# Block sums of a layer's up weights: made by accumulating transfers in DRAM instead of on GpSimd

## The reference, cut to what matters

```
h = h + mx[5] * conv_ffn(modulate(rmsnorm(h, norm2_g[1]), mx[3], mx[4]), w_up[1], conv_w[1], conv_b[1], w_down[1])
```

## Time and profile before

| | |
|---|---|
| time, median of 3 runs | 2627.46 us (2626.0 to 2628.0) |
| the profiled execution, its own time | 2625.86 us |
| its span, first to last instruction | 2624.1 us |
| TensorE busy | 2435.8 us, 93% |
| VectorE busy | 1433.1 us, 55% |
| ScalarE busy | 924.4 us, 35% |
| GpSimd busy | 527.5 us, 20% |
| traffic | 322.33 MB, mean 123 GB/s |
| mean granted TensorE clock | 0.984 of full speed |

### The profile page before, as it was taken

One profiled execution on the slowest core, in us unless ns is written; L12 is line 12 of the kernel. 1 busy time (PEld: TensorE's weight loads), 2 busy tenths in 40 slices (PEclk: granted clock), 3 DMA queues, 4 the chain that ended last, 5 costly groups with the idle time before them and its releaser, 6 DMA issues. The chain is left out here.

```text
span 2624.1 us, 35244 instructions
## 1 busy us (share of the span) xinstructions
PE 2435.8 (93%) x14592; PEld 1884.4 (72%) x14592; DVE 1433.1 (55%) x2132; ACT 924.4 (35%) x1524; POOL 527.5 (20%) x388
## 2 busy tenths in 40 slices
PE   6999999999999999999988878899899999998977
PEld 5887578888887887996667878674664578773323
DVE  4323664766667215226679989536766766532223
ACT  3224433332325114225445555423432653330001
POOL 0502320000001001105247667100013120012112
PEclk9999999999999999999999899999999999999999
DMA  6214901111111212127112222321110114458998
GB/s 241 78 65 142 335 27 60 54 65 65 65 60 45 67 58 79 65 81 272 71 65 81 73 72 76 122 89 74 65 61 10 49 49 145 161 219 352 417 412 331
DMA packets 63248, 322.33 MB, mean 123 GB/s; under 512 B 8109, under 2 KB 20397, under 8 KB 31789
## 3 DMA queue, kind: packets, MB, share of 16 engines
q1 hardware_dynamic: 51374, 300.27, 31.0%
q0 software_dynamic: 5696, 12.59, 1.3%
q10 hardware_dynamic: 6016, 7.18, 0.8%
HBM read 315.82 MB, written 12.58 MB: 125 GB/s over the span
## 5 line engine op out<-in xcount | busy, mean ns | idle before, releaser
L1750 PE MATMUL ps<-work_rounded,ring_rounded 128*128 128x512 f32 (+3 forms) x1968 | 518.4, 351 | 6.0 <-PEq L1555 3.6
L1750 PE MATMUL ps<-xn_rounded,ring_rounded 128*128 128x512 f32 (+3 forms) x2176 | 508.8, 345 | 0.0
L1750 PEld LDWEIGHTS ps<-xn_rounded,ring_rounded 128*128 128x128 f32 (+1 forms) x2176 | 349.2, 189 | 53.5 <-issue 0.5
L1750 PEld LDWEIGHTS ps<-work_rounded,ring_rounded 128*128 128x128 f32 (+1 forms) x1968 | 324.0, 189 | 62.7 <-issue 6.3
L1750 PE MATMUL ps<-big_rounded,ring_rounded 128*128 128x512 f32 (+1 forms) x1168 | 314.9, 356 | 11.3 <-DVE big_rounded L1650 8.7
L1650 DVE TENSOR_TENSOR ring_rounded<-ring,ring_rounded 128x2048 fp32r<-128x2048 f32 (+4 forms) x107 | 192.6, 1800 | 237.4 <-ACT ring_rounded L1614 237.3
L3048 PE MATMUL ps<-xn_rounded,ring_rounded 128*128 128x512 f32 (+1 forms) x1408 | 305.5, 339 | 0.0
L1614 ACT ACTIVATE ring_rounded<-ring 128x2048 fp32r<-128x2048 f32 (+4 forms) x107 | 161.0, 1505 | 309.9 <-PE ps L1750 281.6
L3048 PEld LDWEIGHTS ps<-xn_rounded,ring_rounded 128*128 128x128 f32 x1408 | 218.0, 189 | 30.9
L1750 PEld LDWEIGHTS ps<-big_rounded,ring_rounded 128*128 128x128 f32 x1168 | 190.7, 189 | 53.1 <-DVE big_rounded L1650 12.6
L798 PE MATMUL ps<-xn_rounded,ring_rounded 128*128 128x258 f32 x418 | 128.7, 308 | 35.1 <-DVE h_rounded L978 14.5
(11 more groups left out here) (534 smaller groups left out, 4293.5 us busy)
## 6 DMA issues: line engine op xcount, KB each, us to landing
ring<-in_stream SPq DMA_DIRECT2D x141, 1024.0 KB, 4.9
big<-in_experts SPq DMA_DIRECT2D x44, 1024.0 KB, 24.0
ring<-in_stream SPq DMA_DIRECT2D x32, 704.0 KB, 4.0
ring<-in_experts SPq DMA_DIRECT2D x17, 1024.0 KB, 27.3
xn<-in_experts SPq DMA_DIRECT2D x15, 1024.0 KB, 15.5
work<-in_experts SPq DMA_DIRECT2D x15, 1024.0 KB, 15.3
big<-in_first_modulation SPq DMA_DIRECT2D x8, 1024.0 KB, 14.8
work<-in_bias ACTq DMA_DIRECT2D x20, 256.0 KB, 4.2
```

The source lines that it names most:

```text
L1750: mm = pe.matmul(out[:, a - u.first:b - u.first], lhs, rhs, start=j == 0 and n == 0 and not u.onto, stop=j == terms - 1 and n == len(passe ...
```

## The change

1. The host lays the four blocks of all 22 strips out a second time, block by block (`blocks`, four arrays of 704 x 2048). In layer 0's `ffn_up`, POOL issues eight DRAM-to-DRAM transfers into a new tensor `block_sums`: four copies, then four that add onto what is there. POOL waits for completion three times between them. The scheme is now that of the matrix with its second half negated, so every sum is an addition: `block_sums` holds S1 = A21+A22, S2' = A11+S1, S3' = A11+A21 and S4' = A12+S2'. In return the activation sums T1, T2 and T4 are formed with the opposite sign (`minus_sum`), and the second half is multiplied by -1 where it is evicted.
2. In the stage, POOL makes no sums. SP loads them: a strip comes in three transfers (A11 with A12, A22, and S4' in A21's place), and S1, S2 and S3 in one of 256 KB each, when the product that used their place is done. S2 has two places now, S1 and S3 one.
3. The first half's convolution is held in a PSUM bank (`middle`) instead of SBUF: ACT's `centre` writes it there, DVE's two taps work on it there, `silu` reads it and writes SBUF.
4. The lists of DVE and ACT are in a new order.

```diff
@@ SevenProducts @@
-    def sum_s1(self, pool, n):
...
-        pool.tensor_tensor(self.sums(0, 2), pair(2), pair(3), ALU.add).then_inc(self.sums_made.up(), 1)
...
+    def first_loads(self, sp):
+        sp.wait_ge(b.blocks_summed.sem, b.all_blocks_summed)
+        b.load_strips_until(sp, self.first + 1)
+        for name, n in (("S1", 0), ("S2", 0), ("S3", 0), ("S2", 1)):
+            self.load_sum(sp, name, n)
+    def loads(self, sp):
+        for i in range(FT):
+            if i + 1 < FT:
+                sp.wait_ge(self.done.sem, self.after("P5", i))
+                self.load_sum(sp, "S1", i + 1)
+            if i + 2 < FT:
+                sp.wait_ge(self.done.sem, self.after("P6", i))
+                self.load_sum(sp, "S2", i + 2)
+            b.load_strips_until(sp, self.first + i + 3)
+            if i + 1 < FT:
+                sp.wait_ge(self.done.sem, self.after("P7", i))
+                self.load_sum(sp, "S3", i + 1)
...
     def gpsimd(self, pool):
         self.add_square(pool, KT - 1)
-        self.sum_s1(pool, 1)
-        self.sum_s2(pool, 1)
-        for i in range(FT + 1):
...
+        for i in range(1, FT + 1):
+            if i - 1 < FT - 1:
+                self.add_side(pool, i - 1)
+            if i >= 2:
                 self.gate(pool, i - 2)
...
     def silu(self, act, i):
         act.wait_ge(self.convolved.sem, self.convolved.at(3 * i + 2))
-        act.activation(self.cv[:, i % 2, 0, :], self.cv[:, i % 2, 0, :], ACT.Silu).then_inc(self.silued.up(), 1)
+        if i >= 2:
+            act.wait_ge(self.gated.sem, self.after_gate(i - 2))
+        act.activation(self.cv[:, i % 2, 0, :], self.middle(i), ACT.Silu).then_inc(self.silued.up(), 1)
...
     def make_fourth(self, dve, i):
...
+        if i >= 2:
+            dve.wait_ge(self.silued.sem, self.silued.at(i - 1))
...
     def convolve_first(self, dve, i, part):
-        cc, a = self.cv[:, i % 2, 0, :], 2 * part
+        cc, a = self.middle(i), 2 * part
@@ Builder.load_strips_until @@
+            if i in BLOCK_STRIPS:
+                sp.dma_start(room[:, 0:1024], strip[:, 0:1024]).then_inc(self.landed[slot], 16)
+                sp.dma_start(room[:, 1536:2048], strip[:, 1536:2048]).then_inc(self.landed[slot], 16)
+                sp.dma_start(room[:, 1024:1536], self.sum_of(3, n)).then_inc(self.landed[slot], 16)
+    def sum_blocks(self, pool):
+        for to, block in ((0, 2), (2, 0), (1, 0), (3, 1)):
+            pool.dma_start(sums[to], blocks[block]).then_inc(summed.up(16), 16)
+        pool.wait_ge(summed.sem, summed.now())
+        pool.dma_start(sums[0], blocks[3], accum_op=ALU.add, max_dma_last_dim=4 * STRIP).then_inc(summed.up(16), 16)
+        pool.dma_start(sums[2], blocks[2], accum_op=ALU.add, max_dma_last_dim=4 * STRIP).then_inc(summed.up(16), 16)
+        pool.wait_ge(summed.sem, summed.now())
+        pool.dma_start(sums[1], sums[0], accum_op=ALU.add, max_dma_last_dim=4 * STRIP).then_inc(summed.up(16), 16)
+        pool.wait_ge(summed.sem, summed.now())
+        pool.dma_start(sums[3], sums[1], accum_op=ALU.add, max_dma_last_dim=4 * STRIP).then_inc(summed.up(16), 16)
@@ ffn_up, on GpSimd @@
                 pool.memset(w[:, 0:4 * 772], 0.0).then_inc(zeroed.up(), 1)
+                self.sum_blocks(pool)
```

More of the change, by code:

```diff
@@ L115 @@
 WIDTH = [len(rows) // P * len(cols) for _, rows, cols in PLAN]
+BLOCK_STRIPS = [i for i, (name, _, _) in enumerate(PLAN) if name == ("w_up", DEPTH - 1)]
+TRANSFERS = [3 if i in BLOCK_STRIPS else 1 for i in range(STRIPS)]
 def pack_strip(matrix, rows, cols):
@@ L313, in lay_out @@
     out["first_modulation"] = np.stack([pack_strip(x["w_mod"][0], np.arange(D), np.arange(c, c + 256)) for c in range(0, 256 * MOD_FIRST, 256)])
+    blocks = np.stack([stream[i] for i, (name, _, _) in enumerate(PLAN) if name == ("w_up", DEPTH - 1)])
+    out["blocks"] = blocks.reshape(FT, P, 4, 512).transpose(2, 0, 1, 3).reshape(4, FT * P // 4, STRIP)
     experts = np.empty((EXPERTS, P, 3 * STRIP), np.float32)
@@ L548, in __init__ @@
             lows += [("s4_a22", i - 1)]
-            lows += [("s3", i), ("a12", i)] if i < FT else []
+            lows += [("a12", i), ("s3", i)] if i < FT else []
             lows += [("a11", i + 1)] if i + 1 < FT else []
+        added = [("side", 0)]
+        for i in range(1, FT - 1):
+            added += [("side", i), ("gate", i - 1)]
+        added += [("gate", FT - 2)]
+        self.added_number = {p: n + 1 for n, p in enumerate(added)}
         self.high_number = {p: n + 1 for n, p in enumerate(highs)}
@@ L733, in sum_s3, with load_sum @@
-    def sum_s3(self, pool, n):
-        self.b.strip(pool, self.first + n)
-        if n >= 2:
-            pool.wait_ge(self.done.sem, self.after("P7", n - 2))
-        pair = lambda part: self.slot(n, part).rearrange("p (k c) -> p k c", k=2)
-        pool.tensor_tensor(self.sums(4 + 2 * (n % 2), 2), pair(0), pair(2), ALU.subtract).then_inc(self.sums_made.up(), 1)
-    def sum_s4(self, pool, n):
-        pool.wait_ge(self.sums_made.sem, self.sum_number(n, "S2"))
-        pair = lambda part: self.slot(n, part).rearrange("p (k c) -> p k c", k=2)
-        pool.tensor_tensor(pair(2), pair(1), self.sums(2, 2), ALU.subtract).then_inc(self.sums_made.up(), 1)
+    def load_sum(self, sp, name, n):
+        which = ("S1", "S2", "S3").index(name)
+        place = self.sum_place(name, n)
+        landed = self.sum_landed[name + str(n % 2) if name == "S2" else name]
+        sp.dma_start(self.sums(place, 2), self.b.sum_of(which, n)).then_inc(landed, 16)
@@ L1056, in vector @@
         self.low_a12(dve, 0)
+        self.make_fourth(dve, 0)
         self.low_s3(dve, 0)
@@ L1112, in _ @@
             def _(sp):
-                b.load_strips(sp)
+                self.loads(sp)
             @block.scalar
@@ L2904, in _, with output_projection @@
                 normalise(2)
-    def output_projection(self, src, segments, residual, prefetch=None, add=None, gpsimd=None, next_sources=None, tiles_ahead=0, rooms=None, after=None, waiting=(1, 2)):
+    def output_projection(self, src, segments, residual, prefetch=None, add=None, gpsimd=None, next_sources=None, tiles_ahead=0, rooms=None, after=None, waiting=(1, 2), loads=None):
         width = segments[-1][1]
@@ L2929, in finish @@
             return ins
-        self.project(units, 4, finish, banks_each=2, prefetch=prefetch, add=add, gpsimd=gpsimd, after=after,
+        self.project(units, 4, finish, banks_each=2, prefetch=prefetch, add=add, gpsimd=gpsimd, after=after, loads=loads,
                      following_strip=bool(next_sources), following_halves=bool(next_sources), tiles_ahead=tiles_ahead, waiting=waiting,
@@ L3274, in layer @@
             self.seven = SevenProducts(self, l)
-            self.output_projection(*mixed, add=self.seven.add, after=self.seven.after_eviction, gpsimd=self.seven.on_gpsimd)
+            self.output_projection(*mixed, add=self.seven.add, after=self.seven.after_eviction, gpsimd=self.seven.on_gpsimd, loads=self.seven.first_loads)
         with self.without_border():
```

208 lines of the change are left out of this document (99 added, 109 removed).

## The result

| | before | after |
|---|---|---|
| time, median | 2627.73 us (2626.0 to 2634.41, 4 runs) | 2559.84 us (2556.17 to 2562.68, 4 runs) |
| ratio | | 0.9736, 95% interval 0.9715 to 0.9757 |
| profiled execution, its own time / span | 2625.86 / 2624.1 us | 2559.99 / 2558.2 us |
| TensorE, VectorE, GpSimd busy | 2435.8, 1433.1, 527.5 us | 2415.4, 1341.6, 380.7 us |
| traffic, mean TensorE clock | 322.33 MB, 0.984 | 385.78 MB, 0.988 |

The change makes the kernel 67.9 us faster; 60 were forecast, 2567 us.

A forecast was written before the change was run, and what follows sets the result against it. VectorE, slowed by GpSimd's instructions, was taken to bound the stage of the seven products. 60 (tiles) + 2 (start) - 2 (late strips) = 60 us gained, giving 2567 us; own range 2550 to 2579, 8 in 10 range 2548 to 2606.

The forecast's parts named there:

- What bounds the kernel: Stage of seven products: VectorE sets the pace, slowed by GpSimd; six GpSimd instructions cost it 4.2 us of a tile.
- The free prices that I took: VectorE's durations with GpSimd out of the way: low parts 1.21 and 0.67 us, taps 0.74; 8.85 per tile with evictions, bank sums.
- VectorE's durations: Stage: with four of GpSimd's six instructions removed, VectorE's sum per tile falls to 10.3 us, on the high side.
- The tile: Stage: 13.67 us a tile falls to 10.8, TensorE's 10.1 plus wait; gain over 21 tiles 60 us.
- the wait, for which I chose 0.7: Stage: 0.7 us of wait per tile on top of TensorE's 10.1, as two chains have under a us to spare.
- first rival: Stage: fetch chains set the pace, 12.0 us per tile, gain 35, 2592 us in all; chance 0.19.
- The wait I named as a sign of this rival: Stage: ScalarE waiting for `h` or `ring` to land for more than a us per tile would show fetch chains setting the pace.
- The start: Before the stage's first bank sum: three low parts at slow durations become faster, 2 us gained (0 to 3).
- The sums in DRAM: Layer 0: copies and additions take 270 us, over at about 711, 100 us early; cost zero, covered by GpSimd's idle time.
- second rival: Layer 0: copies crowd out strips, TensorE stands still 39 us at 214 GB/s; 2606 us in all; chance 0.12.
- The 2 us I took off for this: Layer 0: 2 us lost to strips that land later while the DRAM sums are made.
- third rival: Layer 0: additions too slow; at 100 GB/s 206 us late, 2773 us; each us late costs one; chance 0.10.

The follow-up runs named there:

- 4: The kernel before with only the first half convolved in a PSUM bank, GpSimd's sums kept: 2611.59 us, ratio 0.9938.
- 6: The kernel of 4 with GpSimd's sums replaced by additions on unused operands, ScalarE and VectorE waiting for none: 2587.73 us, ratio 0.9849.
- 1: The changed kernel with four unused additions per tile put back on GpSimd at their old places: 2589.7 us, ratio 0.9863.
- 5: The kernel of 1 with the first half's convolution in SBUF instead of a bank: 2607.7 us, ratio 0.9924.
- 3: The changed kernel with the first half convolved in SBUF instead of a PSUM bank: 2556.85 us, ratio 0.9733.
- 12: The changed kernel without bank, with copies in 8 KB rows and ScalarE's copy of the fifth product ahead of A11's high part: 2560.14 us, ratio 0.9729.
- 11: The changed kernel with the four DRAM copies cut into rows of 8 KB instead of some 45 KB: 2556.03 us, ratio 0.9721.
- 10: The changed kernel with one more copy and six more addition rounds on an unread DRAM tensor ahead of the last round: 2592.51 us, ratio 0.9865.
- 7: The changed kernel with VectorE's work in the stage in the order of the kernel before: 2583.4 us, ratio 0.9826.

## Why the prediction was right, point by point

**What bounds the kernel: right.** VectorE set the pace, and GpSimd's additions set how long its instructions took. I put the whole of 13.67 - 10.8 down to durations, and the stretches bear that out: VectorE is busy for 12.46 - 8.44 = 4.02 us a tile less, more than the 3.08 that the tile lost, and the rest is idle time, since TensorE leads now. A path from before to after, each step one run or a pair of them:

| step | us a tile | change | change of VectorE's busy time |
|---|---|---|---|
| before | 13.67 | | |
| + bank (4) | 12.95 | -0.72 | -1.11 |
| + nobody waits, other operands (6) | 11.73 | -1.22 | -1.41 |
| + no additions, new orders (after) | 10.59 | -1.14 | -1.50 |

From the other end, putting additions back costs 1.45 with the bank (1) and 2.09 without it (5). The steps aren't independent (the bank is worth 0.72 with the additions and 0.08 without) and no run has ScalarE's new list alone, so no share belongs to one part of the change. Nor is a step a cause: the second changes the additions themselves as well as the waits.

Did waiting for GpSimd's sums cost anything besides? In the stage of before VectorE waits 3.0 us for a sum and ScalarE 6.2 (line 852), 0.4 us a tile together. No run shows what of that reached TensorE.

**When an instruction collides.** I read the tap of 0.74 us at 1510.69 as one with GpSimd idle. It isn't: GpSimd's line 738 starts 0.04 us after it and runs on beyond its end.

```profile
1510.73 1.87 POOL L738 TENSOR_TENSOR h<-ring 128x512 f32<-128x512 f32 x1 [3.38 <-DMA ring<-in_stream]
```

So running side by side is not enough. Going through the 165 low parts and taps between the first and the last bank sum of before, each with its operands in SBUF: the 101 that start while an instruction of GpSimd is under way all take longer (512 low parts 1.42 to 1.84 us, taps 1.17 to 1.83, 1024 low parts 2.28 to 2.35). The other 64 take 0.67 to 0.68, 0.74 to 0.75 and 1.21 to 1.22, though GpSimd starts beside 21 of them. The free prices that I took are right all the same.

**VectorE's durations.** Forecast 10.3 us a tile with two GpSimd instructions left. After, the groups sum to (61.7 + 40.6 + 31.5 + 15.6 + 15.3 + 15.2 + 9.4 + 9.4)/22 = 9.03 us (the two low-part groups with all their forms). So two instructions of GpSimd take little here. In 3, where the taps are in SBUF, the same groups sum to 10.08 us, 1.23 above the free 8.85: 0.6 for each of the two, near the 0.7 of the forecast. What brings it down to 9.03 is the bank. The exception is the 1024 low part of S4 and A22, 1466 ns against 1.21 us free.

**The tile: 10.8 forecast, 10.59 measured.** TensorE's need was right: from 1351 to 1573 it is busy for 213.75 us, 10.18 a tile, with the clock at 1.00. The mis-sized term is the wait, for which I chose 0.7. In that window two rows are left, 8.2 us or 0.39 a tile; the other waits shown above lie ahead of it and behind it:

```profile
PE ps L814 <- DVE h_rounded L1000: 5.8, 5, 1.8
PE ps L814 <- DVE ring_rounded L1000: 2.4, 4, 0.6
```

So 60 became 64.7.

**The fetch chains (first rival): refuted.** A 256 KB sum lands in 3.1 us, where I took the bias load's 5.2. ScalarE waits 1.7 us in all for S1, S2 or S3. The wait I named as a sign of this rival is there, 24.0 us for the strip's last transfer (line 861, above), over 1 us a tile, and yet 12 removes it and gains nothing. The sign was badly chosen. A wait counts only if it reaches the leading engine. Rate in the stage: 36.23 MB in 210 us, 173 GB/s, 170 forecast.

DMA issues from 1360 to 1570:

```profile
h<-block_sums SPq DMA_DIRECT2D x58, 256.0 KB, 3.1
```

**The start: 2 forecast, 4.7 measured.** TensorE's wait at line 806 of before was 6.5 us (after, 822: 3.8), and its waits of 1.8 and 1.1 us for the first bank sum and a low part are gone. That is 5.6 in all; I had counted only three slow low parts.

**The sums in DRAM: cost zero, right; the time, too high.** Forecast 270 us, measured 626.7 - 442.0 = 185. The four copies moved 23.1 MB in 78 to 80 us, 288 to 296 GB/s, where I took a strip's 214; a single addition took 5.77 MB in 35 to 36 us, 160 to 165 GB/s. With both of its sources read that is 11.5 MB in 36 us, 320 GB/s: about the copies' rate. The Trainium skill (Collectives: The Full Stack, section "The bandwidth ceiling: the fold count and why AG ≠ RS ≠ AR") says of the adding phase of a collective that the add needs two source reads and so halves the rate; 160 against 296 GB/s here agrees.

**Copies crowd out strips (second rival): the mechanism was there, its price wasn't.** During the copies strips landed after 15.7, 26.2 and up to 29.2 us; the rival's figures were 16 at 417 GB/s and 32 at 214. Loss sets in only beyond 25.5 us, the copies lasted 78 us instead of 127, and the two misses cost ScalarE 13.5 us that TensorE never saw. Whether a 45 KB row is one packet was left open: it nearly is, 41 KB (11). The Trainium skill (DMA: Bandwidth & Descriptors, section "Queues, rings and completion order") has the engines take turns packet by packet. 26.2 falling to 11.5 us at an unchanged total rate agrees in direction. In size it doesn't quite: one turn each for 8 KB packets would give a strip half of 333 GB/s, 1 MB in 6.3 us, and it took 11.5. The 2 us I took off for this weren't lost.

**Additions too slow (third rival): refuted by 185 us of room,** and its price, one us per us, is nearly right: 0.8 to 1 (10).

**Behind the stage, 3.5 us lost, not forecast.** The last residual update of layer 1 (line 3236) starts 67.3 us earlier than its twin before, so 2.1 of them go in the down product and 1.4 behind it. What takes them wasn't tried; they are under what the runs tell apart.

## What to carry to other kernels

When an engine sets the pace and another shares its time, look at how long its instructions take when they start beside the other's, and at how long alone. Before you put a difference between two runs down to waiting, compare the leading engine's busy and idle time per tile: in 7 the loss was idle time, in 6 the gain was not. An instruction put back as a load should read what the real one reads; otherwise its price may be another one. Work whose inputs are known from the start can be moved to DMA engines that are idle much earlier in the program, as long as a late finish has room: here 185 us of it, with each us beyond costing 0.8 to 1 us. In this kernel one engine's hand-written list could not go back without the other's (7).

## What the runs showed of the hardware

- An accumulating transfer between DRAM tensors moves 5.77 MB in 35 to 36 us alone (160 to 165 GB/s) and two at once take 67.2 us; plain copies 288 to 296 GB/s.
- A 1 MB load of another queue took 26.2 us instead of 4.9 while copies of 41 KB packets ran, and 11.5 with 8 KB packets.
- A VectorE instruction with both operands in SBUF takes longer if an instruction of GpSimd is under way when it starts (101 of 101 in before), and its free time if GpSimd's starts after it (21 of 21).
- With an operand in PSUM it doesn't collide: a tap on the bank takes 742 ns on the mean beside the six instructions a tile of 4, 749 in 1 and 750 after; in SBUF it takes 1296 beside two (3).
- A fill by GpSimd (526 ns) seems to do VectorE little harm: low parts of 981 and 1034 ns on the mean beside four of them a tile, against 949 and 944 with none.
- TensorE's clock fell to 0.50 (its 1.2 GHz level) where it had stood nearly idle for 20 us (10, from 820), and was at 1.00 through a stage in which it was busy 46 to 50 of 50 us.
